# A hybrid recurrent decoder step on one core: another order of branches at the merge, one barrier without GpSimd, one count for the last product

## The chip, the core and the metric

The program runs on one NeuronCore of a Trainium2 chip. Its time is the device time of one execution in microseconds (us), from the profiler or from timed runs; lower is better. The engines are TensorE (PE in the profile; its weight loads are PEld), VectorE (DVE), ScalarE (ACT), GpSimd (POOL) and SyncE (SP, which here only issues DMAs). Each has its own in-order instruction queue, and they meet through semaphores. SBUF is the on-chip memory of 128 partitions, PSUM holds TensorE's results in eight banks.

## The reference, cut to what matters

1072 tokens (16 meta tokens, 1024 of a prompt, 8 sequences of 4) of width 1024 go through one layer in float32. Four token mixers work side by side on 256 channels each, and their outputs are merged with gates:

```python
o_hg = _head_rms(o_hg, p['hgrn_norm']) * jax.nn.silu(hg)          # branch 0, rows 0 and 1
o_rw = (_head_ln(y_rw, ...) + bonus.reshape(B, T, -1)) * g        # branch 1, rows 2 and 3
o_gl = _head_rms(o_gl, p['gla_norm']) * jax.nn.silu(gg)           # branch 2, rows 4 and 5
o_ml = _head_rms(o_ml, p['mlstm_norm']) * jax.nn.sigmoid(mo)      # branch 3, rows 6 and 7
outs = jnp.stack([o_hg, o_rw, o_gl, o_ml], axis=2).astype(h.dtype)
proj = jnp.einsum('btnc,ncd->btnd', outs, p['w_branch'])
gates = jax.nn.sigmoid(zgate).reshape(B, T, N_BRANCH, D_MODEL)
mix = jnp.sum(proj * gates, axis=2) @ p['w_out']
...
x = x + mix
hn = _rms(x, p['norm_mlp'])
x = x + jnp.square(jax.nn.relu(hn @ p['w_up'])) @ p['w_down']
```

## The kernel before, in words

Activations lie transposed: a "row" is 128 channels by 1056 or 1074 tokens. Every float32 product is made of three matmuls of parts with fewer bits (`split_mm`, lines 545 to 547: high by high, high by low, low by high). So each operand is first split: a copy gives the high part (ScalarE or VectorE), a subtraction on VectorE the low part (`split_lo`, line 629). Tokens are cut into three groups of 352 columns.

The stages run in this order: input projection, mLSTM tiles, GLA and HGRN2 tiles together, RWKV tiles, the merge of the branches, OUT (`w_out`), UP (`w_up`), DOWN (`w_down`). While the mixers' tiles run, TensorE also streams the rest of the input projection; SyncE sends these rows to `Z` in DRAM, the gates among them, and loads the next weight chunk (512 KB) into one of two halves of `RING`. The mixers' outputs of branches 0, 2 and 3 wait in DRAM (`OS`), those of RWKV (rows 2 and 3) in SBUF (`OTR`).

At the end of the RWKV tiles stands barrier 4 (`barrier`, line 484): TensorE, ScalarE, VectorE and GpSimd each drain and count up `phase`; SyncE, ScalarE, VectorE and GpSimd wait for 14. GpSimd first writes the RWKV states out (line 905) and waits for `out`. Then it loads the six rows from `OS` into `HT` (line 917). SyncE, which has loaded two chunks into `RING` for OUT, loads branch weights into `WB` (line 747) and gate rows into `GZ` (line 750).

The merge is a loop over four values of `jj`, each of which makes two rows of the merged sum, `v` = 0 and 1, from four branches each: eight steps `c`. Per step TensorE multiplies two rows by branch weights (18 matmuls, into the three banks of `u` = c % 2), ScalarE takes the sigmoid of a gate row (line 1827), VectorE multiplies the two (`L2592` for the first branch of a sum, `L2597` for the others), and VectorE or GpSimd (line 925) adds to the sum. The product frees the banks (`mul0`, `mul1`) and the gate buffer; SyncE waits for it before it loads the gate row two steps on. Ahead of the loop ScalarE makes the high parts of rows 0 to 7 (`o_hi`, line 1808) and of the first weights (`wb_hi`, line 1815), VectorE the low parts (`o_lo`, `wb_lo`), in the order 0, 1, weights 0, 2 to 7, weights 1; the first sigmoid comes after all of them. `pz` counts finished branches, and starts at 1.

DOWN has four quarters (`jj`) of 32 activation rows. ScalarE and VectorE split one row after the other into two pairs of buffers; TensorE uses a row for 18 matmuls (`down_quarter`, from line 1398) and counts `act_used`, which starts at 2 and lets ScalarE refill a buffer. After every fourth row comes a drain that counts `chunk_done0` or `chunk_done1`, for which SyncE waits before it loads the next weight chunk into that half of `RING`; VectorE splits that chunk after a later row (`split_chunk`). `down0` and `down1` tell VectorE that a quarter's result is complete, and `down_used0` and `down_used1` (line 2804) tell TensorE that VectorE has added it.

Of the kernel before, what the change touches and what calls it, by code (L numbers as in the profile page):

```python
# [142 lines left out]
def build(nc, A, OUT, fcols, ucols, fdim, udim):  # L143
    ctx = ExitStack()
    with ctx:
# [342 lines left out]
        PHASES = {1: 4, 2: 7, 3: 10, 4: 14}  # L488
# [173 lines left out]
        def sp_program(e):  # L662
# [75 lines left out]
            for u in range(2):  # L738
                e.wait_ge(S(f"split{u}"), P_OUT)
                load_chunk(e, P_OUT, u)  # L740
# [10 lines left out]
            for u in range(2):  # L751
                wb(u, u)
                zrow(u, u)

            def branch(jj, first, last):
                for c in range(2 if first else 0, 8):
                    if c % 4 == 2 and not last:
                        e.wait_ge(S(f"wb_split{c // 4}"), jj + 1)
                        wb(jj * 2 + (2 + c // 4), c // 4)
                    e.wait_ge(S(f"mul{c % 2}"), jj * 4 + (c // 2 + 1))  # L760
                    zrow(jj * 8 + c, c % 2)
            branch(0, True, False)
            with e.Fori(1, 3) as jj:
                branch(jj, False, False)
# [27 lines left out]
            def down_quarter(jj, first):  # L792
                for s in range(first, 4):
                    for u in range(2):
                        e.wait_ge(S(f"chunk_done{u}"), jj * 4 + (P_DOWN - P_OUT + 3 + s))
                        down_load(jj, s, u)
# [17 lines left out]
        def pool_program(e):  # L814
# [98 lines left out]
            e.wait_ge(S("out"), 27 * 16)  # L913
            barrier(e, 4)

# [42 lines left out]
        def _(e):  # L958
# [350 lines left out]
            with e.Fori(0, 4) as jj:  # L1309
                for v in range(2):  # L1310
                    e.wait_ge(S(f"wb_split{v}"), jj + 1)
                    for br in range(4):
                        u, c = br % 2, 4 * v + br
                        e.wait_ge(S("o_lo"), 2 * br + 2)
                        e.wait_ge(S(f"mul{u}"), jj * 4 + (c // 2 + 1))
                        for tg in range(3):
                            t = group(tg, True)
                            for k in range(2):
                                r = 2 * br + k
                                last = split_mm(e, PS(3 * u + tg, 0, LGRP), WBH_R[:, v, r, :], WBL_R[:, v, r, :],  # L1320
                                                OT_R[:, r, t], HT_R[:, r, t], k == 0, k == 1)
                        last.then_inc(S("pz"), 1)
# [78 lines left out]
            def down_quarter(jj, rows):  # L1401
                for r in range(rows):
                    q, b = r // 4, r % 2
                    u = q % 2
                    if r % 4 == 0:
                        e.wait_ge(S(f"split{u}"), jj * 4 + (P_DOWN + q // 2 + 1))
                    e.wait_ge(S("act_parts"), jj * 32 + (r + 1))
                    for v in range(2):
                        if r == 0:
                            e.wait_ge(S(f"down_used{v}"), jj + 1)  # L1410
                        for g in range(3):
                            last = down_mm(u, v, r, g, AHI_R[b], ALO_R[b])
                        if r == 31:
                            last.then_inc(S(f"down{v}"), 1)
                    if r < 31:
                        last.then_inc(S("act_used"), 1)
                    else:
                        e.drain().then_inc(S("act_used"), 1)
                    if r % 4 == 3:
                        e.drain().then_inc(S(f"chunk_done{u}"), 1)  # L1420
# [38 lines left out]
        def _(e):  # L1459
# [350 lines left out]
            def wb_hi(jj, v, done=None):  # L1810

                e.wait_ge(S(f"wb{v}"), (jj + 1) * 16)
                if done is not None:
                    e.wait_ge(S("pz"), done)
                e.activation(WBH_R[:, v], WB[:, v], ACT.Copy).then_inc(S("wb_hi"), 1)
            for r in range(2):
                o_hi(r)
            wb_hi(0, 0)
            for r in range(2, 8):
                o_hi(r)  # L1820
            wb_hi(0, 1)

            def branch(jj, more):
                for c in range(8):
                    u = c % 2
                    e.wait_ge(S(f"z{u}"), (jj * 4 + (c // 2 + 1)) * 16)
                    e.activation(late(GZ[:, u]), late(GZ[:, u]), ACT.Sigmoid).then_inc(S("sig"), 1)
                    if c == 4 and more:
# [7 lines left out]
            with e.Fori(0, 3) as jj:  # L1836
# [135 lines left out]
        def _(e):  # L1972
# [595 lines left out]
            def wb_lo(jj, v):  # L2568
                e.wait_ge(S("wb_hi"), jj * 2 + (v + 1))
                split_lo(e, WBL_R[:, v], WBH_R[:, v], WB[:, v]).then_inc(S(f"wb_split{v}"), 1)  # L2570

            def o_lo(r):
                src = OTR[:, r - 2] if r in (2, 3) else HT[:, r]
                e.wait_ge(S("o_hi"), r + 1)
                split_lo(e, late(HT_R[:, r]), late(OT_R[:, r]), late(src)).then_inc(S("o_lo"), 1)
            for r in range(2):
                o_lo(r)
            wb_lo(0, 0)
            for r in range(2, 8):
                o_lo(r)  # L2580
            wb_lo(0, 1)

            e.wait_ge(S("o_lo"), KD)

            def branch(jj, more):
                for c in range(8):
# [6 lines left out]
                    else:  # L2593
# [4 lines left out]
                        if br != 2:  # L2598
# [3 lines left out]
                            e.tensor_tensor(mix, mix, late(GPR[:, br - 1]), ALU.add).then_inc(S("mix_add"), 1)  # L2602
                    if c == 5:
# [14 lines left out]
            with e.Fori(0, 3) as jj:  # L2618
# [180 lines left out]
            def add_residual(k, n, v):  # L2799
                e.wait_ge(S(f"down{v}"), n + 1)  # L2800
# [30 lines left out]
            def end_residual(g):  # L2831
                t = group(g, True)
                for v in range(2):
                    e.wait_ge(S(f"down{v}"), 3 + g + 1)
# [111 lines left out]
```

## Time and profile before

| | us |
|---|---|
| median of three timed runs | 2280.73 (2280.65 to 2280.94) |
| the profiled execution | 2273.0 |
| its span, first to last instruction | 2271.3 |
| TensorE matmuls busy | 2134.3 (94%) |
| VectorE busy | 1265.8 (56%) |
| ScalarE busy | 761.7 (34%) |
| GpSimd busy | 190.8 (8%) |

Stages by the timelines: the RWKV tiles end at about 1280, the merge's matmuls run from 1300 to 1418, OUT and UP follow, and DOWN runs from 1865 to the end.
### The profile page before, as it was taken

Reading aid. Unit: us, or ns where it says so; the run is one execution under the profiler, and the core shown is the slowest. Engines: PE = TensorE matmul, PEld = TensorE weight load, DVE = VectorE, ACT = ScalarE, POOL = GpSimd, SP = SyncE. Lnnn points to the kernel's source line nnn. Section 1 sums busy time; section 2 is a strip of 40 time slices with the busy share of each in tenths; the row PEclk is TensorE's granted clock in tenths of the full one; section 3 lists DMA queues with packets and bytes.
Section 4 is the critical chain, followed back from the end, with each engine's and each line's share of the span. In section 5 each row is a group of like instructions: output and inputs, shape, how many; then the busy total and the mean of one; then the engine's idle time right before and its main releaser. Section 6 shows DMA issues by size and latency. Waiting matters only on the chain.

```text
span 2271.3 us, 34947 instructions
## 1 busy us (share of the span) xinstructions
PE 2134.3 (94%) x13417; PEld 2035.2 (90%) x13417; DVE 1265.8 (56%) x2212; ACT 761.7 (34%) x1252; POOL 190.8 (8%) x335
## 2 busy tenths in 40 slices
PE   4999999999999799999999688999999999999998
PEld 3988888899999799999998587999999999999997
DVE  6424432667775355544543367567666665656566
ACT  5232313224242343334332243023333333333343
POOL 0100011222212200000000111000000002000000
PEclk9999999999999899999998799999999999999999
DMA  4111234222121411211110454332322228111112
GB/s 177 43 51 60 69 43 148 85 65 83 56 89 50 132 51 53 63 50 47 47 45 29 146 175 157 114 113 94 113 88 100 93 83 307 37 46 46 37 47 95
DMA packets 89681, 194.70 MB, mean 86 GB/s; under 512 B 11184, under 2 KB 54144, under 8 KB 89360
## 3 DMA queue, kind: packets, MB, share of 16 engines
q1 hardware_dynamic: 75376, 144.89, 19.6%
q0 software_dynamic: 14208, 48.92, 6.1%
q8 instruction: 43, 0.70, 0.1%
q14 instruction: 22, 0.18, 0.0%
q10 hardware_dynamic: 32, 0.01, 0.0%
HBM read 137.51 MB, written 56.27 MB: 85 GB/s over the span
## 4 chain that ended last, share of the span: by engine, by line
PE 82%; DVE 7%; DMA 4%; ACT 3%; issue 2%; POOL 1%; SPq 0%; DVEq 0%; POOLq 0%; ACTq 0%
PE PS L545 22%; PE PS L546 20%; PE PS L547 20%; PE PS L1091 2%; PE PS L1217 2%; DMA AR<-zrows 2%; PE PS L1208 2%; PE PS L1222 2%; DMA RING<-in_w_all 1%; PE PS L1079 1%; DVE AR L2597 1%; PE PS L1269 1%; ACT AR L1682 1%; PE PS L1115 1%; PE PS L1255 1%
## 5 line engine op out<-in xcount | busy, mean ns | idle before, releaser
L545 PE MATMUL PS<-HT_parts,W_parts 128*128 128x358 f32 (+1 forms) x1440 | 511.2, 355 | 9.1 <-ACT AR L597 5.4
L546 PE MATMUL PS<-OT_parts,W_parts 128*128 128x358 f32 (+1 forms) x1440 | 478.4, 332 | 0.0
L547 PE MATMUL PS<-HT_parts,W_parts 128*128 128x358 f32 (+1 forms) x1440 | 477.0, 331 | 0.0
L545 PEld LDWEIGHTS PS<-HT_parts,W_parts 128*128 128x128 f32 x1440 | 279.1, 194 | 18.0 <-issue 7.0
L546 PEld LDWEIGHTS PS<-OT_parts,W_parts 128*128 128x128 f32 x1440 | 279.1, 194 | 1.8
L547 PEld LDWEIGHTS PS<-HT_parts,W_parts 128*128 128x128 f32 x1440 | 278.8, 194 | 0.0
L545 PE MATMUL PS<-ACT_parts,CF_parts 128*128 128x352 f32 x720 | 236.2, 328 | 12.7 <-issue 7.2
L547 PE MATMUL PS<-ACT_parts,RING_parts 128*128 128x352 f32 x720 | 232.0, 322 | 0.0
L597 ACT ACTIVATE AR<-PS 128x358 f32<-128x358 f32 (+1 forms) x162 | 75.0, 463 | 324.7 <-PE PS L547 324.6
L545 PEld LDWEIGHTS PS<-ACT_parts,CF_parts 128*128 128x128 f32 x720 | 135.4, 188 | 21.1 <-DVE CF_parts L629 11.5
L1947 ACT ACTIVATE ACT_parts<-AR 128x1056 fp32r<-128x1056 f32 x88 | 95.8, 1089 | 167.2 <-PE PS L547 167.2
L603 DVE TENSOR_TENSOR W_parts<-RING,W_parts 128x1024 fp32r<-128x1024 f32 x60 | 73.1, 1218 | 126.6 <-ACT W_parts L590 108.5
L2487 DVE COPY_PREDICATED AR<-CU,PS 128x256 f32<-128x256 uint8 (+2 forms) x93 | 40.0, 485 | 176.0 <-PE PS L1222 145.6
L547 PEld LDWEIGHTS PS<-ACT_parts,RING_parts 128*128 128x128 f32 x720 | 136.0, 189 | 0.0
L546 PE MATMUL PS<-ACT_parts,CF_parts 128*128 128x352 f32 x360 | 116.8, 325 | 0.0
L546 PE MATMUL PS<-CF_parts 128*128 128x352 f32 x360 | 116.2, 323 | 0.0
L545 PE MATMUL PS<-OT_parts,WB_parts 128*128 128x352 f32 x192 | 66.1, 344 | 33.5 <-DVE WB_parts L629 19.8
L629 DVE TENSOR_TENSOR ACT_parts<-AR,ACT_parts 128x1056 fp32r<-128x1056 f32 x44 | 55.4, 1259 | 65.6 <-ACT ACT_parts L1947 65.6
L545 PE MATMUL PS<-UP_parts 128*128 128x352 f32 x256 | 83.8, 327 | 4.4 <-DVE UP_parts L2666 4.4
L2263 DVE COPY_PREDICATED AR<-CU,PS 128x512 f32<-128x512 uint8 (+1 forms) x60 | 61.9, 1031 | 45.9 <-PE PS L1091 43.5
L547 PE MATMUL PS<-UP_parts 128*128 128x352 f32 x256 | 83.7, 327 | 0.0
L546 PE MATMUL PS<-UP_parts 128*128 128x352 f32 x256 | 83.6, 327 | 0.0
(453 smaller groups left out, 4548.3 us busy)
## 6 DMA issues: line engine op xcount, KB each, us to landing
RING<-in_w_all SPq DMA_DIRECT2D x116, 512.0 KB, 3.8
zrows<-AR SPq DMA_DIRECT2D x102, 179.0 KB, 1.9
AR<-zrows SPq DMA_DIRECT2D x32, 528.0 KB, 3.6
act_rows<-AR POOLq DMA_DIRECT2D x24, 528.0 KB, 3.3
AR<-act_rows POOLq DMA_DIRECT2D x24, 528.0 KB, 7.2
zrows<-AR SPq DMA_DIRECT2D x60, 176.0 KB, 1.9
CF<-in_w_all SPq DMA_DIRECT2D x16, 512.0 KB, 4.6
AR<-zrows SPq DMA_DIRECT2D x8, 640.0 KB, 4.6
```

Of the source, the lines that this page charges most:

```text
L545: e.matmul(out, whi, xhi, start=first, stop=False)
L546: e.matmul(out, whi, xlo, start=False, stop=False)
L547: return e.matmul(out, wlo, xhi, start=False, stop=last)
L597: e.activation(ZS[:, g, 0:w], PS(6 + (u + g) % 2, 0, w), func).then_inc(S("gt_free"), 1)
L603: e.tensor_tensor(RLO_R[:, u], RING[:, u], RHI_R[:, u].bitcast(F32), ALU.subtract).then_inc(S(f"split{u}"), 1)
L629: return e.tensor_tensor(lo, x, hi.bitcast(F32), ALU.subtract)
L1091: last = e.matmul(PS(3 * (l % 2), lo * m, hi * m)[0:w], x[:, g, l, 0:w], GQB[:, l % 2, lo * m:hi * m], start=True, stop=True)
L1208: last = e.matmul(PS(4, h * m, h * m + m)[hi], pb[lo, at + hi.start:at + hi.stop], half(ti[:, h * w:h * w + w], lh, False)[lo], start=True ...
L1217: last = e.matmul(PS(0, h * m, h * m + m)[lo], m1[hi, at + lo.start:at + lo.stop], half(tt[:, at:at + w], lh, True)[hi], start=True, stop= ...
L1222: last = e.matmul(PS(1, h * m, h * m + m)[0:w], tt[0:w, h * w:h * w + w], half(m1[0:w, h * w:h * w + w], lh, False), start=True, stop=True)
L1947: e.activation(late(AHI_R[r % 2]), late(act_row(r)), ACT.Copy).then_inc(S("act_hi"), 1)
L2263: ins = e.copy_predicated(dst, bc(half(m, h, True).unsqueeze(1), dst.shape), PS(3 * (l % 2), 0, 4 * w)[0:w].rearrange("p (a n t) -> p a n ...
```

## The change

- The branches are taken in the order 1, 0, 2, 3 (`BRANCHES`), and so the rows in the order 2, 3, 0, 1, 4, 5, 6, 7 (`O_ROWS`), for copies, splits, gates and matmuls. TensorE waits for single rows.
- Barrier 4 counts to 13: GpSimd no longer drains and counts there, and waits for `phase` alone. The wait that the states have been written moves to VectorE, ahead of its first product.
- The first branch weights go to `RING[:, 0]`, and SyncE issues them ahead of its wait for the barrier; the chunk that had been loaded there comes after the first round of the merge.
- SyncE issues the first two gate rows ahead of the second weights.
- In the first round the splits of rows 4 to 7 and of the second weights stand between the first gates' sigmoids and products; this round is written out instead of looped.
- In DOWN the drains are gone. `act_used` counts each row by its last matmul, and SyncE waits for it instead of `chunk_done`; VectorE waits for it instead of `down1`, which now counts only at the end.

```diff
-        PHASES = {1: 4, 2: 7, 3: 10, 4: 14}
+        PHASES = {1: 4, 2: 7, 3: 10, 4: 13}
+        BRANCHES = (1, 0, 2, 3)
+        O_ROWS = [2 * b + k for b in BRANCHES for k in range(2)]
+        def branch_weights(jj, v):
+            return RING[:, 0] if isinstance(jj, int) and jj == 0 and v == 0 else WB[:, v]
@@ SyncE
-            for u in range(2):
-                e.wait_ge(S(f"split{u}"), P_OUT)
-                load_chunk(e, P_OUT, u)
+            e.wait_ge(S("split0"), P_OUT)
+            e.dma_start(RING[:, 0], A["w_br"][0]).then_inc(S("wb0"), 16)
+            e.wait_ge(S("split1"), P_OUT)
+            load_chunk(e, P_OUT, 1)
             e.wait_ge(S("phase"), PHASES[4])
...
-            for u in range(2):
-                wb(u, u)
-                zrow(u, u)
+            def gate(jj, c):
+                zrow(jj * 8 + (c // 4 * 4 + BRANCHES[c % 4]), c % 2)
+            gate(0, 0)
+            gate(0, 1)
+            wb(1, 1)
             def branch(jj, first, last):
                 for c in range(2 if first else 0, 8):
...
                     e.wait_ge(S(f"mul{c % 2}"), jj * 4 + (c // 2 + 1))
-                    zrow(jj * 8 + c, c % 2)
+                    gate(jj, c)
             branch(0, True, False)
+            load_chunk(e, P_OUT, 0)
...
-                        e.wait_ge(S(f"chunk_done{u}"), jj * 4 + (P_DOWN - P_OUT + 3 + s))
+                        e.wait_ge(S("act_used"), jj * 32 + (8 * s + 4 * u - 2))
                         down_load(jj, s, u)
@@ GpSimd
             rw_states(True)
-            e.wait_ge(S("out"), 27 * 16)
-            barrier(e, 4)
+            e.wait_ge(S("phase"), PHASES[4])
@@ TensorE
-                        e.wait_ge(S("o_lo"), 2 * br + 2)
                         e.wait_ge(S(f"mul{u}"), jj * 4 + (c // 2 + 1))
                         for tg in range(3):
                             t = group(tg, True)
                             for k in range(2):
-                                r = 2 * br + k
+                                r = O_ROWS[2 * br + k]
+                                if tg == 0:
+                                    e.wait_ge(S("o_lo"), 2 * br + k + 1)
...
-                        if r == 31:
-                            last.then_inc(S(f"down{v}"), 1)
-                    if r < 31:
-                        last.then_inc(S("act_used"), 1)
-                    else:
-                        e.drain().then_inc(S("act_used"), 1)
-                    if r % 4 == 3:
-                        e.drain().then_inc(S(f"chunk_done{u}"), 1)
+                        if r == 31 and v == 0:
+                            last.then_inc(S("down0"), 1)
+                    last.then_inc(S("act_used"), 1)
@@ ScalarE
-            for r in range(2):
+            o_hi(O_ROWS[0])
+            wb_hi(0, 0)
+            for r in O_ROWS[1:4]:
                 o_hi(r)
-            wb_hi(0, 0)
-            for r in range(2, 8):
-                o_hi(r)
-            wb_hi(0, 1)
             def branch(jj, more):
                 for c in range(8):
...
                     e.activation(late(GZ[:, u]), late(GZ[:, u]), ACT.Sigmoid).then_inc(S("sig"), 1)
+                    if isinstance(jj, int) and jj == 0 and c < 2:
+                        for r in O_ROWS[4 + 2 * c:6 + 2 * c]:
+                            o_hi(r)
+                        if c == 1:
+                            wb_hi(0, 1)
...
-            with e.Fori(0, 3) as jj:
+            branch(0, True)
+            with e.Fori(1, 3) as jj:
                 branch(jj, True)
@@ VectorE
-                e.wait_ge(S("o_hi"), r + 1)
+                e.wait_ge(S("o_hi"), O_ROWS.index(r) + 1)
...
-            for r in range(2):
+            o_lo(O_ROWS[0])
+            wb_lo(0, 0)
+            for r in O_ROWS[1:4]:
                 o_lo(r)
-            wb_lo(0, 0)
-            for r in range(2, 8):
-                o_lo(r)
-            wb_lo(0, 1)
-            e.wait_ge(S("o_lo"), KD)
+            e.wait_ge(S("out"), 27 * 16)
...
+                    if isinstance(jj, int) and jj == 0 and c < 2:
+                        for r in O_ROWS[4 + 2 * c:6 + 2 * c]:
+                            o_lo(r)
+                        if c == 1:
+                            wb_lo(0, 1)
+                            e.wait_ge(S("o_lo"), KD)
...
-                e.wait_ge(S(f"down{v}"), n + 1)
+                e.wait_ge(S("act_used" if v else "down0"), n * 32 + 34 if v else n + 1)
...
-                    e.wait_ge(S(f"down{v}"), 3 + g + 1)
+                    e.wait_ge(S(f"down{v}"), g + 1 if v else 3 + g + 1)
```

## Rows read from the trace of the kernel before

**Rows 1.** The waits, 1262 to 1300 us: engine, line, releaser; us in total, times, longest.
```profile
PE PS L545 <- DVE WB_parts L629: 19.8, 1, 19.8
```

**Rows 2.** The chain that ended last, 1262 to 1300 us: start us, us, what.
```profile
1281.09 2.44 POOLq L484
...
1286.76 13.97 DMA HT<-orows
```

**Rows 3.** The timeline of ScalarE around the seam: start us, us, instruction, [idle before].
```profile
1280.05 0.46 ACT L597 ACTIVATE AR<-PS 128x352 f32<-128x352 f32 x1 [3.71 <-PE PS L547]
1294.84 2.06 ACT L1808 ACTIVATE OT_parts<-HT 128x1056 fp32r<-128x1056 f32 x2 [14.32 <-DMA HT<-orows]
...
1300.76 4.00 ACT L1808 ACTIVATE OT_parts<-HT 128x1056 fp32r<-128x1056 f32 x4 [0.97 <-DMA HT<-orows]
...
1305.73 1.28 ACT L1827 ACT_TABLE_LOAD   x1
```

**Rows 4.** The timeline of SyncE around the seam.
```profile
1280.92 0.93 SPq L606 DMA_DIRECT2D RING<-in_w_all  x2
1283.55 0.33 SPq L747 DMA_DIRECT2D AR<-in_w_br  x1
```

**Rows 5.** The timeline of VectorE in the merge: its products.
```profile
1308.39 1.26 DVE L2592 TENSOR_TENSOR AR<-PS,AR 128x1056 f32 x1 [0.61 <-ACT AR L1827]
1309.57 1.25 DVE L2597 TENSOR_TENSOR AR<-PS,AR 128x1056 f32<-128x1056 f32 x1
...
1314.50 1.26 DVE L2597 TENSOR_TENSOR AR<-PS,AR 128x1056 f32<-128x1056 f32 x1 [2.39 <-ACT AR L1827]
1316.79 1.26 DVE L2597 TENSOR_TENSOR AR<-PS,AR 128x1056 f32<-128x1056 f32 x1 [1.04 <-ACT AR L1827]
...
1337.26 1.25 DVE L2592 TENSOR_TENSOR AR<-PS,AR 128x1056 f32 x1
...
1365.68 1.25 DVE L2592 TENSOR_TENSOR AR<-PS,AR 128x1056 f32 x1
```

**Rows 6.** The chain that ended last, in the merge's third round.
```profile
1368.28 4.71 DMA AR<-zrows
1373.01 1.10 ACT AR L1827
```

**Rows 7.** Line 1420: duration in ns min/median/max, first and last start in us.
```profile
L1420 PEldq DRAIN  x30: 13/3092/3093, 1874.4 to 2229.4; - x30
```

**Rows 8.** The waits of TensorE in DOWN, 1865 to 2235 us.
```profile
PE PS L545 <- issue: 7.5, 26, 0.5
PE PS L545 <- DVEq L2804: 2.9, 3, 1.0
...
PE PS L545 <- DVE CF_parts L629: 1.0, 1, 1.0
```

**Rows 9.** The timeline of TensorE over one boundary in DOWN.
```profile
1901.65 0.32 PE L547 MATMUL PS<-ACT_parts,RING_parts 128*128 128x352 f32 x1
1902.21 0.42 PE L545 MATMUL PS<-ACT_parts,CF_parts 128*128 128x352 f32 x1 [0.24 <-issue]
1902.47 0.32 PE L546 MATMUL PS<-CF_parts 128*128 128x352 f32 x1
```

**Rows 10.** The timeline of VectorE at the same boundary.
```profile
1900.37 1.25 DVE L629 TENSOR_TENSOR CF_parts<-AR,ACT_parts 128x1056 fp32r<-128x1056 f32 x1
```

**Rows 11.** GpSimd's DMA queue in 1286:1288, then 1290:1292: packets, MB, share of 16 engines.
```profile
q0 software_dynamic: 4, 0.02, 2.0%
...
q0 software_dynamic: 112, 0.41, 51.1%
```

**Rows 12.** The timeline of TensorE in the merge's first branch.
```profile
1300.18 0.49 PE L546 MATMUL PS<-HT_parts,WB_parts 128*128 128x352 f32 x1
...
1304.58 0.43 PE L546 MATMUL PS<-HT_parts,WB_parts 128*128 128x352 f32 x1
```

**Rows 13.** Busy us (instructions) of PE, PEld, DVE, ACT, POOL; PEclk, DMA share, GB/s.
```profile
1340.00:1345.00 5.00, 5.00 (x26) 5.00 (x25) 2.22 (x2) 1.69 (x2) 0.04 (x1) 0.77 0.57 199
```

More of the change, by code:

```diff
@@ L1814, in wb_hi @@
                     e.wait_ge(S("pz"), done)
-                e.activation(WBH_R[:, v], WB[:, v], ACT.Copy).then_inc(S("wb_hi"), 1)
-            for r in range(2):
+                e.activation(WBH_R[:, v], branch_weights(jj, v), ACT.Copy).then_inc(S("wb_hi"), 1)
+            o_hi(O_ROWS[0])
+            wb_hi(0, 0)
+            for r in O_ROWS[1:4]:
                 o_hi(r)
-            wb_hi(0, 0)
-            for r in range(2, 8):
-                o_hi(r)
-            wb_hi(0, 1)
             def branch(jj, more):
@@ L2569, in wb_lo @@
                 e.wait_ge(S("wb_hi"), jj * 2 + (v + 1))
-                split_lo(e, WBL_R[:, v], WBH_R[:, v], WB[:, v]).then_inc(S(f"wb_split{v}"), 1)
+                split_lo(e, WBL_R[:, v], WBH_R[:, v], branch_weights(jj, v)).then_inc(S(f"wb_split{v}"), 1)
             def o_lo(r):
                 src = OTR[:, r - 2] if r in (2, 3) else HT[:, r]
-                e.wait_ge(S("o_hi"), r + 1)
+                e.wait_ge(S("o_hi"), O_ROWS.index(r) + 1)
                 split_lo(e, late(HT_R[:, r]), late(OT_R[:, r]), late(src)).then_inc(S("o_lo"), 1)
-            for r in range(2):
+            o_lo(O_ROWS[0])
+            wb_lo(0, 0)
+            for r in O_ROWS[1:4]:
                 o_lo(r)
-            wb_lo(0, 0)
-            for r in range(2, 8):
-                o_lo(r)
-            wb_lo(0, 1)
-            e.wait_ge(S("o_lo"), KD)
+            e.wait_ge(S("out"), 27 * 16)
             def branch(jj, more):
@@ L2617, in branch @@
                         split_chunk(e, c - 1, P_OUT)
-            with e.Fori(0, 3) as jj:
+            branch(0, True)
+            with e.Fori(1, 3) as jj:
                 branch(jj, True)
```

## The prediction

> **What bounds the kernel now.** I read the waits around the end of the RWKV tiles first, then the chain there, then the engines' timelines through the merge, and last the waits and timelines of DOWN. TensorE works almost everywhere, so only its idle time is to be had. The change touches two places where it idles.
>
> The first is the seam between the last RWKV tile and the merge. TensorE stands still for 19.8 us until the first split of the branch weights exists [rows 1]. The chain runs through GpSimd: its drain ahead of the barrier takes 2.44 us and ends at 1283.53, then it issues the loads of the `HT` rows, and the chain waits 13.97 us for them [rows 2]. ScalarE evacuated the last stream group at 1280.05 (0.46 us), got its first row pair at 1294.84 and the last four at 1300.76, and turns to the gates' sigmoid only at 1305.73, after all eight rows and both weight copies [rows 3]. So the first product of the merge stands at 1308.39 [rows 5]. After that the merge is paced by a loop, not by TensorE: a gate row takes 4.71 us from DMA, its sigmoid 1.10 [rows 6], the product 1.26 [rows 5]. That is 7.1 us per two branches, 28.3 per round of eight, and the rounds start at 1337.26 and 1365.68, 28.4 apart [rows 5]. A product that comes earlier in the first round therefore shifts everything behind it.
>
> The second is DOWN. Every fourth row of activations ends with a drain on TensorE's queue (30 of them [rows 7]), and at 26 boundaries TensorE idles for no releaser, 7.5 us together [rows 8].
>
> **DOWN, term by term.** Steady matmuls start 0.16 us apart (0.32 us long, half overlapped). Over a boundary the starts are 1901.65, 1902.21, 1902.47: 0.56 + 0.26 in place of 0.32, a loss of 0.50 [rows 9]. The view of waits counts only 0.29 idle each (7.5 / 26); to that belong the lost overlap, 0.16, and the slow second start, 0.10. Together 7.5 + 26 x 0.26 = 14.3 us. With the increments on the last matmul of each row, TensorE does not have to run empty. What is late next is VectorE: at each boundary it splits a weight chunk first and then the next row. That row's split ends at 1900.37 + 1.25 = 1901.62 [rows 10]; an unbroken TensorE would load its next weights at about 1901.65. The chain that leads there (a row's last matmul, ScalarE's copy, VectorE's) hangs on TensorE's own progress, so it moves along with it and the margin stays near nothing. Bounds for what stays at a boundary: 0 (the split is 0.03 early) and 0.50 (the wait costs as much as the drain). I take 0.10, the price of the slow second start, since the rows put the release within 0.1 of the need: 2.6 us. DOWN gains 14.3 - 2.6 = 11.7.
>
> Four boundaries give nothing. At the three quarter ends TensorE waits for `down_used0` (2.9 us, 3 times), at one more for a split row behind a sum of squares (1.0) [rows 8]. VectorE's order sets both; the double drain in front is hidden there. The new thresholds are equivalent: `act_used` starts at 2, so 32jj + 8s + 4u - 2 asks for 32jj + 8s + 4u - 4 finished rows, the end of the chunk that sat in the buffer before. SyncE issues its loads when it did, and `down1`'s replacement fires with the same matmul.
>
> **The seam, step by step.** Without GpSimd the barrier is complete when ScalarE's last evacuation and TensorE's drain are, about 1280.7. SyncE issues the first weights (now into `RING[:, 0]`) and one chunk at 1280.92, where it issued two chunks [rows 4]; then two gate rows and the second weights from 1283.55, where these loads stand now [rows 4]: the barrier goes, but the last sends of `Z` still have to land. ScalarE copies row 2 at 1281.3 to 1282.3 (it lies in SBUF), then waits for the first weights: 4 to 5 us after issue, 1285.6. Copy 1.04 to 1286.6, VectorE's split 1.22 to 1287.8. TensorE starts the RWKV branch at 1287.9 instead of 1299.72, 11.8 us earlier. This is not the gain, as the products wait for more.
>
> GpSimd issues the `HT` loads at about 1281.3 instead of 1284.09; their packets began just before 1288 (4 of them in 1286 to 1288 [rows 11]), 3.7 us after the issue, so now about 1285. While SyncE's queue has work too, GpSimd's gets half of the engines (51.1%, 0.41 MB in 2 us [rows 11]), so the first pair again takes 7 us from its first packet: 1292.2 (1294.84 less about 1287.8, plus 1285.2). The later rows do not gain so much. The engines are full from 1284 on and the bytes before the last `HT` row are the same, six transfers of SyncE and six of GpSimd: one chunk is gone, but the next round's weights, which SyncE issues behind the first weights' split, move up with it from about 1299.6 to 1287.9. Landing 1300.2, from 1300.74. The Trainium skill (DMA: Bandwidth & Descriptors, Issuing engines are not separate DMA queues) says that transfers from several engines interleave on the same DMA engines and that issuing elsewhere saves only issue time. By that rule the last rows land as I have them; were the queues independent they would land 2.8 us earlier, 1297.9, and the gain below would be 2.3 more. The trace bears the rule out (51.1%).
>
> From there ScalarE and VectorE are in order. Rows 0 and 1 copied by 1294.4, the table load 1.28 and the first sigmoid 1.09: 1296.8, first product 1296.9 (was 1308.39). Second product: rows 4 and 5 copied by 1302.3, sigmoid 1303.4, VectorE done with their splits at 1303.8, product at 1303.8 (was 1309.57). Third: the sum to 1306.3, splits of rows 6 and 7 to 1308.8, weights to 1310.0, product at 1310.1, against 1314.50. Fourth: TensorE has its rows at 1308.8 and needs 2.6 to 4.4 us, product between 1311.4 and 1313.3, against 1316.79 [rows 5]. Gains of 4.4 and of 3.5 to 5.4; the later products of both banks follow these by the loop. I take 4.4. Against it stands the chunk for `RING[:, 0]`, now loaded between rounds 0 and 1 among gate rows: 512 KB at about 400 GB/s (0.41 MB in 2 us on half of the engines [rows 11]), 1.3 us at worst, 0 where the sigmoid has slack. I take 0.5. Net 3.9. Bounds: 0 (the stages behind are reached no earlier) and 9 (the loop starts with its first product, 1308.39 - 1296.9 = 11.5, less what VectorE's five splits cost).
>
> Unseen costs: one more body of the merge's loop on three queues, and eight finer waits per half round on TensorE. Waits between rows in DOWN leave no gap where nothing is drained, so zero for them; the body between zero and 0.5 us, I take zero. The order of branches itself costs nothing; operands and sizes are the same.
>
> **Sum.** 11.7 + 3.9 = 15.6 us. The profiled execution took 2273.0 us (span 2271.3), so 2257.4 for it. The runs' median is 2280.73, 7.7 us above; I subtract the same 15.6: 2265.1.
>
> **Rivals.**
> A. VectorE takes the drain's place. For it: a margin of 0.03 us. Against it: its release needs only a queue's reaction, where the drain waits for the matmuls to end and then refills. If all of 0.40 to 0.50 comes back, DOWN gives about 1 and the total is 4.9: 2275.8. Chance 0.12.
> B. The seam gives nothing: the earlier rows land later, or the first round runs at the half clock, and by the second round VectorE stands where it stood. For it: full DMA engines, and a third of the products already lie behind VectorE. Against it: the loop of 7.1 us has no slack to take back a lead. 2280.73 - 11.7 = 2269.0. Chance 0.17.
> C. The seam gives the 9 us of its bound: 2260.0. Chance 0.05.
> D. Slower: TensorE stays at its lower clock through the merge. The clock is at 1.2 GHz after the seam (starts 0.29 us apart [rows 12]) and fell again in the second round after a gap of 2.7 us, 0.77 granted [rows 13]. The change makes the first round a series of short bursts with pauses of 2 to 4 us. At 1.2 GHz a branch takes 18 x 0.293 = 5.3 us, a round 42.2 instead of 28.4, so a round costs 13.8 us and one round at that clock eats DOWN's gain. Two make 2280.73 - 11.7 + 27.6 = 2296.6. Against it: a TensorE that bound the round would no longer pause, and after the seam it had 2.4 GHz back at 1304.6, 5 us after its first matmul [rows 12]. Chance 0.04. The Trainium skill (TensorE: Matmul & The Clock Gate, HAM oscillation) warns of this: short bursts between DMA waits return to the low clock each time. By that rule the time is D's; the trace shows both the fall and the quick return.
>
> **How the numbers follow.** Forecast 0.62, A 0.12, B 0.17, C 0.05, D 0.04. The likeliest is 2265.1; its own range 2259 to 2271 (what stays at a boundary 0 to 0.25, the seam 0 to 7). With B and the better part of A: 2258 to 2275. A change of 0.2% (4.6 us) is about what a measurement tells from none. Faster: forecast, B, C and half of A, 0.90. Within: the rest of A, 0.06. Slower: D, 0.04.
>
> **What would show it.** Starts over DOWN's boundaries 0.2 to 0.3 us apart where they were 0.56, and 26 idles for no releaser gone; the three quarter ends unchanged at about 1 us. The first merge matmul near 1288, the first product near 1297, the fourth near 1312, the second round's first product near 1333 instead of 1337.26, and round 2 again 28.4 us later. Wrong if the boundaries now show as long waits for `CF_parts` by VectorE (A), if the second round starts at 1337 (B), or if the clock through the merge is granted at half for more than 5 us at a time (D).

## The result, and the profile after

The changed kernel's median was 2256.35 us (2252.26 to 2258.36, four runs) against 2280.84 (2280.65 to 2280.99) for the kernel before: ratio 0.989, 95% interval 0.9873 to 0.9908. That is 24.5 us or 1.1% less; the forecast was 15.6 less, and 2256.35 lies below its range. The profiled executions differ by less: 2273.0 against 2256.0 (span 2254.3), 17.0 us.

Two landmarks divide an execution well: the end of the last evacuation before the barrier ("the seam", 1280.51 before), and the first matmuls of OUT and of DOWN. The first fence shows the landmarks of the kernel before that [rows 3] lack, the second those of the changed one (start us, us, instruction, idle before).

```profile
1418.46 0.40 PE L545 MATMUL PS<-MIXH_parts,CF_parts 128*128 128x352 f32 x1 [2.55 <-issue]
1865.60 0.42 PE L545 MATMUL PS<-ACT_parts,CF_parts 128*128 128x352 f32 x1 [1.55 <-DVE HT L2723]
```

```profile
1282.36 0.46 ACT L603 ACTIVATE AR<-PS 128x352 f32<-128x352 f32 x1 [3.70 <-PE PS L553]
...
1414.78 0.40 PE L551 MATMUL PS<-MIXH_parts,CF_parts 128*128 128x352 f32 x1 [2.57 <-issue]
...
1861.91 0.42 PE L551 MATMUL PS<-ACT_parts,CF_parts 128*128 128x352 f32 x1 [1.55 <-DVE HT L2740]
```

From the seam to OUT it was 1418.46 - 1280.51 = 137.95 us, and is 1414.78 - 1282.82 = 131.96. From DOWN to the end of the span it was 2271.3 - 1865.60 = 405.70, and is 2254.3 - 1861.91 = 392.39. Between them nothing moved (447.14 and 447.13). So the profiled pair holds 6.0 at the seam and 13.3 in DOWN, less 2.3 because this execution reached the seam later, before any changed line.

The waits at the seam, as in [rows 1], and GpSimd's and SyncE's issues there:

```profile
PE PS L551 <- DVE WB_parts L635: 8.5, 1, 8.5
...
POOL HT L928 <- ACTq L484: 2.5, 1, 2.5
```

```profile
1283.15 3.21 POOL L928 DMA_DIRECT2D HT<-orows  x6 [2.47 <-ACTq L484]
```

```profile
1283.22 0.43 SPq L746 DMA_DIRECT2D RING<-in_w_br  x1
...
1285.08 1.56 SPq L758 DMA_DIRECT2D AR<-zrows  x2
...
1322.26 0.44 SPq L612 DMA_DIRECT2D RING<-in_w_all  x1
```

TensorE waits 8.5 us where it waited 19.8, and GpSimd is now released by ScalarE's queue, 0.3 us after the seam. Then ScalarE and VectorE, as in [rows 3, 5]:

```profile
1292.12 2.06 ACT L1815 ACTIVATE OT_parts<-HT 128x1056 fp32r<-128x1056 f32 x2 [1.92 <-DMA HT<-orows]
1294.19 1.28 ACT L1832 ACT_TABLE_LOAD   x1
...
1302.38 2.06 ACT L1815 ACTIVATE OT_parts<-HT 128x1056 fp32r<-128x1056 f32 x2 [5.81 <-DMA HT<-orows]
1304.35 1.07 ACT L1832 ACTIVATE AR<-AR 128x1056 f32<-128x1056 f32 x1
```

```profile
1296.67 1.26 DVE L2601 TENSOR_TENSOR AR<-PS,AR 128x1056 f32<-128x1056 f32 x1 [1.01 <-ACT AR L1832]
...
1305.84 1.25 DVE L2606 TENSOR_TENSOR AR<-PS,AR 128x1056 f32<-128x1056 f32 x1
...
1311.78 1.25 DVE L2606 TENSOR_TENSOR AR<-PS,AR 128x1056 f32<-128x1056 f32 x1
1314.02 1.26 DVE L2606 TENSOR_TENSOR AR<-PS,AR 128x1056 f32<-128x1056 f32 x1 [0.99 <-PE PS L553]
...
1333.84 1.25 DVE L2601 TENSOR_TENSOR AR<-PS,AR 128x1056 f32 x1
...
1362.05 1.25 DVE L2601 TENSOR_TENSOR AR<-PS,AR 128x1056 f32 x1
```

The second sigmoid follows the last rows by 2 us, where the first followed them by 6.3 [rows 3]. The last HT rows are there 19.6 us after the seam (20.2 before), the second product follows them by 3.5 us instead of 8.8, and the lead stays: the second round starts 51.0 us after the seam (56.75 before), the third 28.2 later. TensorE's first merge matmul stands at 1290.72, 7.9 us after the seam (19.2 before).

DOWN, as in [rows 8, 9, 10]: TensorE's waits, one boundary with its weight loads, and VectorE there. The first fence ends with a line of the kernel before that [rows 8] lack.

```profile
PE PS L551 <- DVEq L2822: 2.9, 3, 1.0
...
PE PS L551 <- DVE MIXH_parts L635: 1.0, 1, 1.0
PE PS L551 <- DVE CF_parts L635: 1.0, 1, 1.0
...
PE PS L545 <- DVE MIXH_parts L629: 0.6, 1, 0.6
```

```profile
1896.68 0.32 PE L553 MATMUL PS<-ACT_parts,RING_parts 128*128 128x352 f32 x1
1896.84 0.32 PE L551 MATMUL PS<-ACT_parts,CF_parts 128*128 128x352 f32 x1
1897.00 0.32 PE L552 MATMUL PS<-CF_parts 128*128 128x352 f32 x1
```

```profile
1896.52 0.19 PEld L553 LDWEIGHTS PS<-ACT_parts,RING_parts 128*128 128x128 f32 x1
1896.73 0.19 PEld L551 LDWEIGHTS PS<-ACT_parts,CF_parts 128*128 128x128 f32 x1
1896.84 0.19 PEld L552 LDWEIGHTS PS<-CF_parts 128*128 128x128 f32 x1
```

```profile
1895.42 1.25 DVE L635 TENSOR_TENSOR CF_parts<-AR,ACT_parts 128x1056 fp32r<-128x1056 f32 x1
```

The 26 idles by "issue" are gone. A row starts 0.16 us after the last one, even this one, whose split ended at 1896.67. The trace shows how close that is: the row's first weight load starts at 1896.73, 0.06 us behind the split's end and 0.21 behind the load before it, where loads otherwise follow each other by 0.16. The next load follows it by 0.11, so that the second matmul, at 1897.00, is on time again.

What stays are the three quarter ends and the row behind a sum of squares, as forecast, and one wait that grew. In the last quarter VectorE puts another sum of squares between the splits of rows 24 and 25, and TensorE waits 1.0 us for row 25 (`MIXH_parts`), where it waited 0.6. Below, the first row is TensorE's, the next two are VectorE's.

```profile
2217.55 0.42 PE L551 MATMUL PS<-MIX_parts,CF_parts 128*128 128x352 f32 x1 [1.04 <-DVE MIXH_parts L635]
...
2215.07 1.25 DVE L516 TENSOR_TENSOR HT<-HT 128x1056 f32<-128x1056 f32 x1
2216.24 3.59 DVE L635 TENSOR_TENSOR MIXH_parts<-AR,MIX_parts 128x1056 fp32r<-128x1056 f32 x3
```

What the drain ahead of row 24 had cost, some 0.5 us, came back there in full.

### The profile page after: what moved, and what is told of

It is laid out like the page before. It is cut to its first block, busy times and chain, and to the rows that moved or that the text cites. A ratio compares the mean times of both kernels' runs of the same rounds, so it can differ in the third digit from the quotient of the medians.

```text
span 2254.3 us, 34907 instructions
## 1 busy us (share of the span) xinstructions
PE 2128.5 (94%) x13417; PEld 2036.5 (90%) x13417; DVE 1264.1 (56%) x2212; ACT 759.6 (34%) x1250; POOL 191.0 (8%) x335
## 4 chain that ended last, share of the span: by engine, by line
PE 83%; DVE 7%; DMA 4%; ACT 3%; issue 2%; POOL 1%; SPq 0%; DVEq 0%; ACTq 0%; POOLq 0%
PE PS L551 22%; PE PS L552 21%; PE PS L553 21%; PE PS L1102 2%; PE PS L1228 2%; PE PS L1219 2%; PE PS L1233 2%; DMA RING<-in_w_all 1%; DMA AR<-zrows 1%; PE PS L1090 1%; ACT AR L1689 1%; PE PS L1280 1%; DVE AR L2606 1%; DMA HT<-orows 1%; PE PS L1126 1%
```

## The experiments

Seam to OUT and DOWN are read from the profile of each run as above. They repeat far better than whole executions. In the later sessions, on four chips, 60 executions of the kernel before took 2267.8 to 2277.8 us.

**1. Each part alone, and both kernels again.** `e1` has only the DOWN part, `e2` all the rest; `e3` and `e4` are the unchanged kernels.

```diff
-                        e.wait_ge(S(f"chunk_done{u}"), jj * 4 + (P_DOWN - P_OUT + 3 + s))
+                        e.wait_ge(S("act_used"), jj * 32 + (8 * s + 4 * u - 2))
...
-                    if r % 4 == 3:
-                        e.drain().then_inc(S(f"chunk_done{u}"), 1)
...
```

> Only the DOWN part of the change on the kernel before: no drains, one count. The profiled executions differ by 17.0 us (2273.0 to 2256.0), the timed medians by 24.5 (2280.84 to 2256.35). Theory 1 (the two parts add up, and the 7.5 us on top belong to DOWN: in ordinary executions the drains cost more than in the profiled one): 2280.8 - 13.3 - 7.5 = 2260. Theory 2 (the 7.5 us belong to the seam or to TensorE's clock around it): 2280.8 - 13.3 = 2267.5. By my forecast's term for DOWN, 11.7, it would be 2269.1. The profile should show the 26 boundaries without a gap, and the seam as before.

> Everything but the DOWN part: branch order, row splits, weights in the chunk buffer, barrier without GpSimd; DOWN with its drains. Theory 1 (the extra 7.5 us belong to DOWN): the seam gives what the profiles show, about 5.7 us: 2275. Theory 2 (they belong to the seam or to the clock around it): 2280.8 - 5.7 - 7.5 = 2267.6. My forecast's term for the seam was 3.9: 2276.9.

> The kernel before, unchanged, as a kernel of its own: does its profiled execution come out at 2273 again while the timed ones stand at 2280.8, and in which stage do executions of one and the same program differ? Theory P (the profiled execution is faster by chance of TensorE's clock windows): some executions near 2273 appear, and the stages that differ are those with a low granted clock. Theory Q (taking the profile itself changes it): the profiled one is at 2273 again, every timed one at 2280.8.

> The changed kernel, unchanged: its spread (2252.3 to 2258.4 in four runs) against that of the kernel before (0.3 us). Theory P: its executions spread over some 6 us again, with the stretches at the lower clock in other places each time. Theory Q: timed runs and profiled run agree, 2256.

| | median us | ratio to before, 95% | seam at | seam to OUT | DOWN |
|---|---|---|---|---|---|
| before, in these sessions | 2275.61 | | | | |
| before again (e3) | 2273.58 | 0.9982 to 1.0002 | 1283.97 | 135.72 | 405.37 |
| DOWN only (e1) | 2259.96 | 0.9917 to 0.9958 | 1281.09 | 137.22 | 392.49 |
| the rest only (e2) | 2269.42 | 0.9964 to 0.9983 | 1286.70 | 130.33 | 405.47 |
| after again (e4) | 2255.69 | 0.9901 to 0.9934 | 1279.60 | 130.99 | 392.46 |

The parts add: by the medians 15.7 and 6.2 alone and 19.9 together, by the stages 13.07 and 6.05, together 19.1. DOWN is 405.4 to 405.7 us with the drains and 392.4 to 392.5 without. Seam to OUT is 135.7 to 138.0 with the old code (three profiles, mean 137.0) and 130.0 to 132.0 in all eight profiles with the new (mean 130.9).

The extra 7.5 us of the first session did not appear here at all, in neither part and not in the whole, so theories 1 and 2 could not be told apart. Of the other pair, theory Q falls: the timed runs of before stand at 2268 to 2278, around their profile. Theory P holds for that spread: executions of one program reach the seam between 1279.6 and 1286.7 us, and the granted clock up to it was 0.97 in e4 and e1 (seam at 1279.6 and 1281.1) and 0.96 in e2 (1286.7). It does not explain why the first session's four runs of before all stood within 0.3 us of 2280.8.

**2. What gains at the seam.** Four edits taken back or added one at a time, on the changed kernel.

```diff
# e5: GpSimd in the barrier
-        PHASES = {1: 4, 2: 7, 3: 10, 4: 13}
+        PHASES = {1: 4, 2: 7, 3: 10, 4: 14}
-            e.wait_ge(S("phase"), PHASES[4])
+            e.wait_ge(S("out"), 27 * 16)
+            barrier(e, 4)
# e6: the old order
-        BRANCHES = (1, 0, 2, 3)
+        BRANCHES = (0, 1, 2, 3)
# e7: first weights in WB, after the barrier
-            e.dma_start(RING[:, 0], A["w_br"][0]).then_inc(S("wb0"), 16)
+            load_chunk(e, P_OUT, 0)
...
+            wb(0, 0)
...
             branch(0, True, False)
-            load_chunk(e, P_OUT, 0)
# e8: two loads behind the HT rows
-            load_chunk(e, P_OUT, 1)
             e.wait_ge(S("phase"), PHASES[4])
...
-                    if c % 4 == 2 and not last:
+                    if c % 4 == 2 and not last and not (first and c == 2):
...
+                    if first and c == 3:
+                        e.wait_ge(S("wb_split0"), 1)
+                        wb(2, 0)
             load_chunk(e, P_OUT, 0)
+            load_chunk(e, P_OUT, 1)
```

> The changed kernel with GpSimd back in barrier 4 (it drains and counts, the others wait for 14). The stretch from the last evacuation of the RWKV stage to the first matmul of OUT ('seam to OUT') is 131.0 to 132.0 us in the changed kernel and 135.7 to 138.0 before. Theory B (the bytes bound the seam: the DMA engines are full until the last HT row has landed, whenever GpSimd issues): the loads start 3.2 us later, the last row lands under 1 us later, seam to OUT under 133, total within 1 us of the changed kernel (2255.7 on this chip). Theory G (GpSimd's start sets it): seam to OUT +3.2, 2259.

> The changed kernel with BRANCHES = (0, 1, 2, 3), the old order; single-row waits, weights in the chunk buffer, barrier and interleaved splits as changed. TensorE's first matmul then waits for HT rows 0 and 1: about 1298 instead of 1290.7. Theory S (the gain comes from splits standing behind the first sigmoids, the order matters little, as the second product waits for rows 4 to 7 anyway): seam to OUT +1 at most, 2256.5. Theory R (RWKV's rows first are what gains): seam to OUT back to 136 to 138, 2261.

> The changed kernel with the first branch weights in WB again, loaded after the barrier, and the first OUT chunk ahead of it. TensorE starts the first branch some 3 us later, which by both theories is hidden, since the first product waits for rows 0 and 1. Theory B (bytes bound the seam): 512 KB more ahead of the last HT row at 400 GB/s, so it lands 1.3 us later, seam to OUT +1.3, 2257. Rival: no change beyond noise, since the bytes are not what decides.

> The changed kernel with two 512 KB loads taken from in front of the HT rows: the second OUT chunk goes behind the first round of the merge, and the weights of round 1 behind the gate row of step 3. Theory B (bytes bound the seam): the last HT row lands 2.6 us sooner (about 19.5 - 2.6 = 17 us after the last evacuation), every product from the second on is 2 to 2.6 us sooner, 2253.3. Rival: the loads moved behind collide with the gate rows of the loop and take it back: 2256.

| | median us (before there: 2273.39) | last HT rows after the seam | seam to OUT |
|---|---|---|---|
| changed kernel (eight profiles) | | 18.9 to 19.6 | 130.0 to 132.0 |
| GpSimd in the barrier (e5) | 2257.04 | 20.7 | 131.91 |
| old order (e6) | 2254.66 | 18.9 | 130.42 |
| weights after the barrier (e7) | 2256.19 | 19.4 | 131.12 |
| fewer bytes (e8) | 2252.79 | 16.5 | 128.08 |

None of the first three, taken back alone, moves seam to OUT out of the changed kernel's range. In e5 GpSimd issues 3.4 us later against the seam (1286.19, seam 1282.48) and the last rows land 1.2 to 1.8 later. TensorE's first merge matmul stands 12.7 us after the seam in e6 and 13.9 in e7, for 7.9; the second product hides both.

The 1.3 us that I expected in e7 did not come, and the run could not show them, because its edit moves no bytes on balance. The weights of round 1 are now issued 13.7 us after the seam instead of 7.7, since they wait for the first weights' split. From the seam to the last landing the changed kernel, e7 and e8 move:

```profile
DMA packets 2010, 7.10 MB, mean 362 GB/s; under 512 B 224, under 2 KB 358, under 8 KB 2010
...
DMA packets 2002, 7.09 MB, mean 367 GB/s; under 512 B 219, under 2 KB 347, under 8 KB 2002
...
DMA packets 1625, 5.73 MB, mean 345 GB/s; under 512 B 176, under 2 KB 304, under 8 KB 1625
```

Fewer bytes did gain: in e8, and in e12 and e15 of part 4, which share that edit, ScalarE gets the last rows 16.4 to 16.8 us after the seam, 2.6 sooner in the mean, and seam to OUT falls by 2.7 (127.8 to 128.6). ScalarE in e8:

```profile
1286.47 0.46 ACT L603 ACTIVATE AR<-PS 128x352 f32<-128x352 f32 x1 [4.67 <-PE PS L553]
...
1303.46 2.06 ACT L1818 ACTIVATE OT_parts<-HT 128x1056 fp32r<-128x1056 f32 x2 [3.52 <-DMA HT<-orows]
```

That leaves the interleave. `e9` puts the splits of rows 4 to 7 and of the second weights ahead of the first sigmoid and product again.

```diff
-            for r in O_ROWS[1:4]:
+            for r in O_ROWS[1:]:
                 o_hi(r)
+            wb_hi(0, 1)
...
```

VectorE's `o_lo` and `wb_lo` move in the same way.

> The changed kernel with the interleave undone: ScalarE and VectorE split rows 4 to 7 and the second weights ahead of the first sigmoid and product, as before; order, buffer and barrier stay changed. Three edits taken back one at a time (barrier, order, buffer) have each left seam to OUT at 130.4 to 131.9, so theory I: the interleave is what gains at the seam, and without it the first two products stand behind all splits: last HT row + 8.8 us for the second product as before, where it is + 3.5 now; seam to OUT 136 to 137, total 2260. Rival: the gain is spread over all edits, seam to OUT 132 to 133.

Measured: 2260.81 us, seam (1285.04) to OUT 136.84. Theory I holds. The timelines of ScalarE and VectorE in e9:

```profile
1304.25 4.00 ACT L1815 ACTIVATE OT_parts<-HT 128x1056 fp32r<-128x1056 f32 x4 [8.02 <-DMA HT<-orows]
1308.15 1.04 ACT L1822 ACTIVATE WB_parts<-AR 128x1024 fp32r<-128x1024 f32 x1
1309.21 1.28 ACT L1833 ACT_TABLE_LOAD   x1
```

```profile
1311.80 1.26 DVE L2599 TENSOR_TENSOR AR<-PS,AR 128x1056 f32<-128x1056 f32 x1 [0.54 <-ACT AR L1833]
1312.97 1.25 DVE L2604 TENSOR_TENSOR AR<-PS,AR 128x1056 f32<-128x1056 f32 x1
```

The second product stands 8.7 us behind the last rows, as in the kernel before. TensorE's first merge matmul stands at 1292.65, 7.6 us after the seam, so it is as early as in the changed kernel. So with order, barrier and buffer changed and this one edit missing, no gain at the seam is left. The interleave is needed for the whole gain; whether it would do alone, with the other three all taken back, no run shows.

**3. The margin in DOWN.** VectorE is delayed between the chunk split and the next row's split: by four memsets of one column (e10), by one reduction (e13), by three (e14). `PAD` is a buffer of 8 columns that nothing reads.

```diff
                         split_chunk(e, q % 2, jj * 4 + (P_DOWN + q // 2), ROUNDS)
+                        for x in range(n):      # n = 1 (e13), 3 (e14)
+                            e.tensor_reduce(PAD[:, 2 * x:2 * x + 1], ones, AX.X, ALU.add)
```

> The changed kernel with four short memsets (one column each, some 0.3 us together) on VectorE behind each chunk split in DOWN, so ahead of the next row's split. My forecast took the margin at the 26 boundaries as near nothing and charged 0.10 us each, and the profile shows no pause there at all. Theory M (the margin is near nothing, but free as long as it is not negative): the delay shows in full, 26 x 0.3 = 8 us, gaps before the first matmul of each fourth row. Rival (there is slack of some tenths that the timelines hide): no gap, DOWN 392.4 us as before.

> The changed kernel with one short reduction (128 columns, about 0.2 us) on VectorE between the chunk split and the next row's split in DOWN. Theory M (the margin is a few hundredths): each of the 26 boundaries waits 0.1 to 0.2 us and restarts with one slow pair, DOWN 392.4 + 26 x 0.25 = 399. Rival (slack of some tenths): DOWN stays at 392.4 to 393.2.

> The same with three such reductions (about 0.6 us). Theory M: DOWN 399 + 26 x 0.4 = 409. Rival (slack of 0.3 to 0.5): 26 x 0.2 to 0.3, DOWN 398 to 400. The difference to the run with one is free of the size of the margin and shows the price per tenth of delay.

The memsets overlapped what stood around them and delayed the row's split by 0.03 us: no boundary paused, DOWN was 393.18, and the run decided nothing. One reduction shifts it by 0.20 (1895.32 to 1895.52), three by 0.58 (1894.96 to 1895.54); DOWN is 397.53 and 408.78. At 30 places these are 0.17 and 0.55 us each: between the two, lateness is paid one for one, 11.25 / (30 x 0.38) = 0.99, and the margin is 0.20 - 0.17 = 0.03. At a paused boundary in e13, matmuls, then weight loads:

```profile
1896.60 0.32 PE L554 MATMUL PS<-ACT_parts,RING_parts 128*128 128x352 f32 x1
1896.82 0.43 PE L552 MATMUL PS<-ACT_parts,CF_parts 128*128 128x352 f32 x1
1897.09 0.33 PE L553 MATMUL PS<-CF_parts 128*128 128x352 f32 x1
```

```profile
1896.82 0.19 PEld L552 LDWEIGHTS PS<-ACT_parts,CF_parts 128*128 128x128 f32 x1 [0.19 <-DVE CF_parts L636]
1896.93 0.19 PEld L553 LDWEIGHTS PS<-CF_parts 128*128 128x128 f32 x1
```

Of the 0.17 us the row's first matmul is late by only 0.06 (0.22 for 0.16), and the slow second start (0.27) makes the other 0.11. That says which matmul the margin belongs to. The split ends at 1896.77 here, and the second matmul starts 0.32 behind it; in e14 it is 0.32 too (1896.79 and 1897.11). In the changed kernel an unbroken stream puts the second matmul 0.35 behind the split's end at most boundaries (1885.04 and 1885.39 at row 8) and 0.33 at the one shown. So the margin is 0.03 or less, and it is the second matmul's: the first alone could take 0.13 (it starts 0.18 behind the split's end at row 8, and 0.05 in e13).

**4. Towards a better version.** `e11` moves the chunk split a row ahead, `e12` adds that to e8, `e15` takes e8 and moves one sum of squares; `e16` is the changed kernel again.

```diff
# e11, e12
-                    if r % 4 == 3 and not (r < 7 and first) and not (r == 31 and last):
+                    if r % 4 == 2 and not (r < 6 and first) and not (r == 30 and last):
# e15
-        SQ_AT = (8, 11, 14, 17, 20, 23)
+        SQ_AT = (8, 11, 15, 17, 20, 23)
```

> The changed kernel with VectorE's chunk split in DOWN one row earlier (after r % 4 == 2 instead of 3). Theory: what is left at the boundaries is VectorE's order. The gap at row 16 of the last quarter (1.12 us) and at row 24 (1.2) go, and the three quarter ends (1.1 each) shrink, since the sum's addition no longer stands behind a chunk split: DOWN 392.4 - 2.3 - 1 to 3 = 387 to 389, total 2251 to 2253. Rival: the chunk has not landed a row earlier, VectorE waits for it, and DOWN gets longer.

> The earlier chunk split together with the two loads taken from in front of the HT rows (seam to OUT 128.1). The two lie in different stages and should add: 2252.8 less what the earlier split gives, 2248 to 2250, faster than both kernels.

> Fewer bytes ahead of the HT rows, and the third sum of squares one row later (r = 15 for 14 in SQ_AT), so that VectorE has it after row 16's split and not between chunk split and row split. The gap of 1.28 us at row 16 of the last quarter goes: DOWN 391.3; seam to OUT 128. Total 2255.7 - 3.4 - 1.1 = 2251.2, against 2252.8 without the second edit. Rival: the sum of squares only moves the wait, to row 17 or to row 24: 2252.8.

> The changed kernel unchanged, five rounds, beside the others. 2255.7 on this scale, spread 2252 to 2258, and the kernel before 2271 to 2278, so a gain of 19 to 20 us: the stages' 13.1 + 5.9. If instead the gain of the first session (24.5) appears, the kernel before must stand near 2280.8 again, and what differs lies ahead of the seam.

The earlier chunk split made DOWN 9 us longer (401.42 and 401.73; medians 2262.13 and 2259.74): the rival was right. VectorE stands in front of a chunk that has not landed, and the rows queue behind it. Its timeline in e11:

```profile
1902.61 0.69 DVE L632 CAST CF_parts<-RING 128x1024 fp32r<-128x1024 f32 x1 [1.92 <-DMA RING<-in_w_all]
1903.34 1.23 DVE L635 TENSOR_TENSOR RING_parts<-RING,CF_parts 128x1024 fp32r<-128x1024 f32 x1
1904.48 1.25 DVE L635 TENSOR_TENSOR ACT_parts<-AR,ACT_parts 128x1056 fp32r<-128x1056 f32 x1
```

VectorE waits so four times (5.3 us). TensorE idles behind three of them, and at row 19 of the last quarter, where chunk split and sum of squares now both stand ahead of the row's split: 4.6 us, 5.7 with the slow restarts, while the boundaries give back 2.3. The rest falls in the last quarter. There the fourth of VectorE's waits is for a chunk ahead of row 27; TensorE idles 2.8 us for that row, and then starts its next matmuls 0.29 us apart at a granted clock of 0.50:

```profile
2223.32 0.66 PE L551 MATMUL PS<-MIX_parts,CF_parts 128*128 128x352 f32 x1 [2.84 <-DVE MIXH_parts L635]
...
2223.30:2229.10 5.80, 5.78 (x20) 5.78 (x21) 4.64 (x4) 0.00 (x0) 0.00 (x0) 0.50 0.00 0
```

Together that tail costs 5.6 us, so that 5.7 - 2.3 + 5.6 makes the 9.0.

The sum of squares worked: DOWN 391.51 (-0.9), seam to OUT 128.56, median 2252.22, ratio 0.9905 (0.9891 to 0.9919). The changed kernel beside it: 2256.31, 0.992 (0.9906 to 0.9933), the kernel before 2274.72. e15 is the fastest here, by 4.1 us in the medians, 3 us by the stages.

## Why the prediction was wrong

- **What bounds the two places**: right. The products of the merge set its length, not TensorE, and a lead in the first round stayed to the end. In DOWN the drains cost what was read from [rows 8, 9].
- **"I take 0.10" for what stays at a boundary, 2.6 us**: mis-sized. At 25 of 26 boundaries at most 0.04 us stayed. At one (row 24 of the last quarter) nothing was gained: the wait for row 25 grew by what the drain had cost, some 0.5. So the 14.3 was right but for that one place, and DOWN gave 13.1 (13.3 in the profiled pair), not 11.7. The margin of 0.03 us agrees with what the delays show, in part by luck: I read it between the split's end and the first weight load, and that load does wait; what must not be late is the second matmul. The slow second start belongs to a wait that happens, not to one that is merely close.
- **"I take 4.4", less 0.5 for the moved chunk, at the seam**: mis-sized, 6.1 in place of 3.9. I took the third product's lead for the loop's. Measured against the seam, the second leads by 6.0, the third by 5.0 and the sixth by 5.7. The moved chunk, issued at 1322.26, cost nothing that shows: e7, which leaves it in its old place, has 131.12 from seam to OUT, the changed kernel 130.0 to 132.0. The landings of the last rows came as forecast (1300.2 + 2.3 for the later seam, measured 1302.38); the first pair came 2.4 us sooner than forecast, and that bought nothing, as the second product waits for the last rows.
- **"I subtract the same 15.6" from the median**: this step put the time out of range. It carries a gain read from one profiled execution over to a median that stood 7.7 us above it. With both terms right (19.3 in the profiled pair) it gives 2261.4, inside my range and still 5.1 above the measured median. The first session's kernel before stood at 2280.8; in the later sessions it stood at 2273.4 to 2275.6, while the changed kernel stayed at 2255.7 to 2256.4. There the change is worth 18.4 and 19.9 us, and the stages account for 19.1. The remaining 4.6 to 6.1 us of the first session's 24.5 are not explained. Executions do differ ahead of the seam, where the stretches at the lower clock lie in other places, but 60 later ones never reached 2280. Whether the first session's chip was another is not on record, so the cause stays open.
- **Rivals**: none of the four happened as a whole; A happened at one boundary of 26. By my own sign for D (half the clock for more than 5 us at a time) D should have come true: from 1301.5 to 1310.5 the granted clock was 0.50. It had been 0.50 from 1285 to 1304 before the change as well. The price was small, since TensorE had pauses left (its matmuls were busy for 5.6 of these 9 us): VectorE waited 0.99 us for TensorE ahead of the fourth product, at 1314.02; at the other products of the first round it waited for ScalarE or for nothing. At 1312 the clock was back.
- **The DMA engines**: in e5 GpSimd issues 3.4 us later and the last rows land only 1.2 to 1.8 later. The Trainium skill (DMA: Bandwidth & Descriptors, Issuing engines are not separate DMA queues) says that DMAs run on the same 16 engines and interleave, whichever engine issued them. The trace agrees: up to the last landing SyncE's queue took 51.8% of the engines and GpSimd's 41.1%.

```profile
1301.50:1310.50 9.00, 5.60 (x18) 5.32 (x19) 6.97 (x6) 6.90 (x7) 0.00 (x0) 0.50 0.29 94
1312.00:1333.00 21.00, 19.71 (x120) 19.13 (x118) 15.49 (x14) 8.32 (x8) 4.53 (x2) 1.00 0.71 227
...
1285.00:1304.00 19.00, 4.28 (x15) 4.28 (x16) 7.97 (x7) 8.19 (x9) 2.32 (x5) 0.50 0.86 323
...
q1 hardware_dynamic: 1131, 3.84, 51.8%
q0 software_dynamic: 879, 3.26, 41.1%
```

The first two lines are of the changed kernel, as in [rows 13], the third of the kernel before, and the last two, as in [rows 11], of the changed kernel from 1282.8 to 1302.4.

## What to carry to other kernels

When an in-order engine prepares several operands ahead of a loop, put each preparation right in front of the step that needs it. Without that the 6 us here were gone, though every other edit at the seam stood, and though TensorE still started its first merge matmul 11 us earlier. A drain that only carries a second count can be replaced by arithmetic on one counter; what it saves is the whole gap, as long as the next release is not late. Where it is late, as behind the sum of squares, the next wait takes the saving. Size a change by stages between landmarks of the profile, and compare executions of one session: whole executions of the kernel before spread over 10 us in the later sessions, and its medians there lay 5 to 7 us below that of the first.

## What had not been expected

- A split that ends 0.03 us ahead of the need costs nothing. The weight load behind it already starts late, which the view of waits does not list. Beyond that each 0.1 us of lateness costs 0.1 us, between delays of 0.20 and 0.58.
- The program takes up to 7 us more or less to reach the same point (1279.6 to 1286.9 us for the seam), with UP behind it equal to within 0.1 us (352.8 to 352.9 in every profile).
- GpSimd's loads: the last pair landed only 1.2 to 1.8 us later when issued 3.4 us later, but 2.6 us earlier with 1 MB less ahead and beside it on SyncE's queue.
- Half the clock for 9 us of the merge's first round shows as one wait of 1 us on VectorE, since TensorE was busy for only 5.6 of them.
